# A transformer block with routed experts on one core: the router's logits taken from rows before their norm, with a shift row fetched by way of DRAM

## The reference, cut to what matters

```python
    mod = (jax.nn.silu(c) @ w_ada + b_ada)[:, None, :]
    sh1, sc1, gt1, sh2, sc2, gt2 = jnp.split(mod, 6, axis=-1)
    ...
    merged = jax.nn.sigmoid(ga) * (ya @ w_branch_a) + jax.nn.sigmoid(gbm) * (yb @ w_branch_b)
    x = x + gt1 * (merged @ w_out)
    h2 = _rmsnorm(x, norm2_g) * (1.0 + sc2) + sh2
    x = x + gt2 * _moe(h2, router_w, router_b, w_gate_up, b_gate_up, w_down, b_down)
```

```python
    logits = (xt @ router_w + router_b).astype(jnp.float32)
    top_v, top_e = lax.top_k(logits, TOP_K)          # 4 of 32 experts
    wts = jax.nn.softmax(top_v, axis=-1)
    ...
        hgu = xb @ w_gate_up[e] + b_gate_up[e]
        gate, up = jnp.split(hgu, 2, axis=-1)
        ...
        return act @ w_down[e] + b_down[e]
    out = jax.ops.segment_sum(ys * pw[:, None].astype(ys.dtype), ptok, num_segments=N + 1)[:N]
```

## Time and profile before

| | us |
|---|---|
| median of 3 runs | 1346.19 |
| lowest and highest | 1345.65, 1347.37 |
| the profiled execution's own time | 1347.94 |
| its span | 1346.2 |
| TensorE busy | 1320.4 (98%) |
| GpSimd busy | 703.6 (52%) |
| VectorE busy | 478.4 (36%) |
| ScalarE busy | 300.9 (22%) |
| HBM read | 482.40 MB, 359 GB/s over the span |

### The profile page before, as it was taken

How to read it: one execution, slowest core, us unless ns; L and a number is a source line. 1 busy time by engine, 2 the same in 40 slices (tenths; PEclk the granted TensorE clock), 3 DMA queues, 4 the chain that set the end, 5 groups by cost and what they waited for, 6 DMA issues and landing times.

```text
span 1346.2 us, 18076 instructions
## 1 busy us (share of the span) xinstructions
PE 1320.4 (98%) x6683; PEld 620.1 (46%) x6684; DVE 478.4 (36%) x862; ACT 300.9 (22%) x577; POOL 703.6 (52%) x430
## 2 busy tenths in 40 slices
PE   7999999999999999999999999999999999999996
PEld 3888545788844333333333333333333333333332
DVE  1160006355578324223233242333332333233332
ACT  2320004310023222222122122222222222222222
POOL 1000000010015777767777687777777777777771
PEclk9999999999999999999999999999999999999998
DMA  9735333499959999999999999999999999999995
GB/s 339 279 127 186 125 125 125 161 322 367 329 219 382 429 428 429 428 403 429 428 428 428 428 409 429 428 428 428 407 431 428 428 428 407 430 428 428 428 427 231
DMA packets 70818, 483.79 MB, mean 359 GB/s; under 512 B 7270, under 2 KB 7466, under 8 KB 44970
## 3 DMA queue, kind: packets, MB, share of 16 engines
q1 hardware_dynamic: 69250, 478.20, 86.8%
q0 software_dynamic: 1056, 3.93, 1.0%
q10 hardware_dynamic: 488, 1.33, 0.3%
HBM read 482.40 MB, written 1.05 MB: 359 GB/s over the span
## 4 chain that ended last, share of the span: by engine, by line
DMA 56%; PE 34%; POOL 4%; issue 3%; DVE 1%; SPq 1%; ACT 1%; POOLq 0%; DVEq 0%; ACTq 0%
DMA landing<-in_w_gate_up 41%; PE bank L1332 15%; DMA landing<-in_w_down 14%; PE bank L1341 6%; POOL gu_slot L566 3%; PE bank L1688 3%; PE bank L1738 3%; PE bank L1574 2%; DMA piece<-in_w_ada 2%; SPq L397 1%; PE bank L1660 1%; PE bank L1553 0%; PE bank L1478 0%; PE bank L1705 0%; SPq L391 0%
## 5 line engine op out<-in xcount | busy, mean ns | idle before, releaser
L566 POOL COPY gu_slot<-landing 128x2048 f32<-128x2048 f32 x246 | 458.8, 1895 | 145.0 <-issue 107.9
L1688 PE MATMUL bank<-gu_slot,xg 128*64 128x512 f32 x2304 | 509.4, 593 | 3.2 <-POOL gu_slot L566 2.8
L1688 PEld LDWEIGHTS bank<-gu_slot,xg 128*64 128x64 f32 x2304 | 164.3, 137 | 320.5 <-issue 298.4
L566 POOL COPY dn_slot<-landing 128x2048 f32<-128x2048 f32 x120 | 223.5, 1894 | 71.2 <-issue 53.6
L1738 PE MATMUL bank<-dn_slot,actT 128*64 128x512 f32 x1152 | 255.1, 595 | 0.0
L1332 PE MATMUL bank<-hT,piece 128*128 128x256 f32 x704 | 153.4, 379 | 0.0
L1738 PEld LDWEIGHTS bank<-dn_slot,actT 128*64 128x64 f32 x1152 | 79.5, 137 | 159.2 <-issue 158.7
L1332 PEld LDWEIGHTS bank<-hT,piece 128*128 128x128 f32 x704 | 133.4, 190 | 19.1 <-issue 1.1
L812 ACT ACTIVATE ypart<-bank 128x512 bf16<-128x512 f32 x105 | 62.7, 597 | 313.8 <-DVE bank L1241 260.2
L1230 DVE TENSOR_SCALAR bank<-bank 128x512 f32<-128x512 f32 x36 | 25.2, 700 | 283.6 <-PE bank L1688 283.6
L1241 DVE SCALAR_TENSOR_TENSOR bank<-bank,slot_w,gt2q 128x512 f32<-128x512 f32 x35 | 26.6, 759 | 238.8 <-PE bank L1738 238.8
(11 more groups left out here) (342 smaller groups left out, 986.8 us busy)
## 6 DMA issues: line engine op xcount, KB each, us to landing
landing<-in_w_gate_up SPq DMA_DIRECT2D x123, 2048.0 KB, 10.7
landing<-in_w_down SPq DMA_DIRECT2D x60, 2048.0 KB, 10.7
piece<-in_w_in SPq DMA_DIRECT2D x17, 2048.0 KB, 7.7
piece<-in_w_ada SPq DMA_DIRECT2D x12, 2048.0 KB, 13.2
gu_slot<-in_w_gate_up SPq DMA_DIRECT2D x10, 1024.0 KB, 7.1
dn_slot<-in_w_down SPq DMA_DIRECT2D x8, 1024.0 KB, 13.8
piece<-in_w_branch_a SPq DMA_DIRECT2D x2, 2048.0 KB, 9.3
piece<-in_w_branch_b SPq DMA_DIRECT2D x2, 2048.0 KB, 8.1
```

Of the source, the lines that this page charges most:

```text
L566: nc.gpsimd.tensor_copy(place, landing[j // 2 % 3][:, j % 2, :]).then_inc(there, 16)
L1688: ins = M(gu_bank[u][64 * q:64 * q + 64, :], xg[:, k % 4, 64 * (k // 4):64 * (k // 4) + 64], gu_slot[k][:, cols_], start=(k == 0), stop=(k ...
```

## The change

Three things are changed together.

1. The logits. TensorE transposes `u`, the row times `sc2g` before the norm (for the first tile a buffer of its own, `u0`), and multiplies it with the router's weights. VectorE multiplies the outcome with 1/rms and adds `cb`, a row of 32 numbers that is the same for all tokens: the shift row sh2 times the router's weights, plus the router's bias. For `cb` GpSimd writes sh2 (one row) to DRAM and reads it back with one element per partition and column (`shc`); TensorE forms the row `hc` from it in the place of `ab6`, and repeats it on all partitions beside the gate sum.
2. The gate row gt2 is formed in one tile (`ab7`) with its two 512-wide halves on the two halves of the partitions, straight into `gt2q`; `gt2`, `ab6` and GpSimd's two copies go. `bd`, the down biases, is kept in that form too and is half as wide.
3. The order. VectorE clears most of its buffers and splits the first tile ahead of the last w_out tile (two of the clearings go to GpSimd); the first block's ranks come in two tiles of their own (`rank0_full`, `rank1_full`), its selection for each token tile apart; the second tile's `h2` is formed behind the logits; `chosen2` of the first block ahead of the router weights, both of which stand behind `br`; the second tile's first subtraction behind the places, its second behind `table`. The products nobody reads are spread over other waits. SyncE's unit 0 waits for the second logits, unit 1 for `h2`; the first two landing buffers change places.

The diff, cut to its core:

```diff
-    + [("wb2", "V"), ("wb3", "V"), ("ab6", "V"), ("wo0", "V"), ("wo2", "V"), ("ab7", "V"), ("wo1", "V"), ("wo3", "V")]
-    + [("hh0", "A"), ("hh1", "A"), ("rp0", "A"), ("rl0", "V"), ("hh2", "A"), ("hh3", "A"), ("rp1", "A"), ("rl1", "V"), ...
+    + [("wb2", "V"), ("wb3", "V"), ("hc", "V"), ("wo0", "V"), ("wo2", "V"), ("ab7", "V"), ("wo1", "V"), ("wo3", "V")]
+    + [("hh2", "A"), ("hh0", "A"), ("hh1", "A"), ("hh3", "A"), ("rp0", "A"), ("rl0", "V"), ("rp1", "A"), ("rl1", "V"), ...
...
 SyncE
+            wait_tile(sp, "rl1")
+            land(E - 1, 0)
             sp.wait_ge(h2_ready, 4)
-            sp.wait_ge(gate_ready, 3)
-            land(E - 1, 0)
-            wait_tile(sp, "rl1")
+            sp.wait_ge(gate_ready, 1)
             land(E - 1, 1)
...
 GpSimd
+            wait_out(pool, "ab3")
+            pool.dma_start(shift_store[:], sh2[0:1, :]).then_inc(shift_out, 16)
+            pool.wait_ge(shift_out, 16)
+            pool.dma_start(shc[:], shift_store[0].rearrange("(k p) -> p k", p=P), allow_slow_non_contiguous=True).then_inc(shc_in, 16)
...
-            for q in range(2):
-                step.settle()
-                step(nc.gpsimd.tensor_copy(gt2q[64 * q:64 * q + 64, :], gt2[64 * q:64 * q + 64, 512 * q:512 * q + 512]), gate_ready)
-            step(nc.gpsimd.tensor_tensor(bd[:], bd[:], gt2[:], ALU.mult), gate_ready)
+            step(nc.gpsimd.tensor_tensor(bd[:], bd[:], gt2q[:], ALU.mult), gate_ready)
+            wait_tile(pool, "wo3")
+            for i in range(2):
+                step(nc.gpsimd.memset(ypart[i][:], 0.0), ypart_ready[i])
...
 VectorE
             weigh(7)
-            take_sum(6)
             take_wo(0)
             take_wo(2)
-            take_sum(7)
-            second_norm(0)
+            take_gate()
+            dve.wait_ge(row_full, 1)
+            step(V.tensor_copy(cb[:], tile("hc")[:, 64:64 + E]), row_out)
+            step.settle()
+            norm_scale(0)
+            norm_rows(0)
...
-                chain(V.tensor_copy(lg[:, t, 0:E], tile(f"rl{t}")[:, 0:E]), out_dve)
+                chain(V.scalar_tensor_tensor(lg[:, t, 0:E], tile(f"rl{t}")[:, 0:E], rs[:, t:t + 1], cb[:], ALU.mult, ALU.add), out_dve)
...
-            router_weights(0)
+            dve.wait_ge(rank0_full, 1)
+            first_slots(0, bank[6][:, 0:1])
+            norm_rows(1)
+            dve.wait_ge(rank1_full, 1)
+            first_slots(1, bank[5][:, 0:1])
             wait_tile(dve, "rt")
...
-            router_weights(1)
+            chosen_of_slots(first_slot[:, 0:1], first_slot[:, 1:2])
             wait_tile(dve, "br")
...
-            subtract_part(0, 1)
+            router_weights(0)
+            router_weights(1)
...
-            subtract_part(1, 1)
+            subtract_part(0, 1)
...
             chain(V.tensor_copy(table[:], tile("te")[0:1, 0:ends[5]]), tables_ready)
+            subtract_part(1, 1)
...
 TensorE
+            pe.wait_ge(late_in, 48)
+            pe.wait_ge(shc_in, 16)
+            ps = begin("hc")
+            for k in range(KT):
+                M(ps[0:1, 0:E], shc[:, k:k + 1], wr[:, k, :], start=(k == 0), stop=False)
+            full(M(ps[0:1, 0:E], ones[0:1, 0:1], rb[:], start=False, stop=True))
             pe.wait_ge(merged_ready, 4)
...
                 if t == 0:
-                    add_parts(7)
+                    add_gate_parts()
+                    wait_out(pe, "hc")
+                    M(tile("hc")[:, 64:64 + E], ones[0:1, :], rb2[:], start=True, stop=True).then_inc(row_full, 1)
...
+            pe.wait_ge(u_ready, 3)
+            transposes("hh2", h2, 1, 0)
+            pe.wait_ge(row_out, 1)
+            transposes("hh0", u0, None, 0)
+            transposes("hh1", u0, None, 1)
+            wait_out(pe, "wo2")
+            keep_busy(bank[7], 4)
+            pe.wait_ge(u_ready, 4)
+            transposes("hh3", h2, 1, 1)
...
-            gate_up(16, 1, (block_tables, weight_transposes))
+            gate_up(16, 1, (weight_transposes, block_tables))
```

More of the change, by code:

```diff
@@ L500, in _ @@
             pool.dma_start(sc2g[:], norm2_g[0:1, :].to_broadcast([P, D])).then_inc(g2_in, 16)
-            for part, dst in ((2, gt1), (3, sh2), (5, gt2), (4, fgb)):
+            for q in range(2):
+                a = 5 * D + 512 * q
+                pool.dma_start(gt2b[64 * q:64 * q + 64, :], b_ada[0:1, a:a + 512].to_broadcast([64, 512])).then_inc(brow_in, 16)
+            for part, dst in ((2, gt1), (3, sh2), (4, fgb)):
                 pool.dma_start(dst[:], b_ada[0:1, part * D:(part + 1) * D].to_broadcast([P, D])).then_inc(brow_in, 16)
@@ L1129, in _ @@
             step(V.memset(selT[:], 0.0), selw_out)
-            for i in range(3):
-                step(V.memset(ypart[i][:], 0.0), ypart_ready[i])
+            step(V.memset(ypart[2][:], 0.0), ypart_ready[2])
             step(V.memset(zrow[:], 0.0), zrow_ready)
+            subtract_part(1, 0)
             dve.wait_ge(numbers_ready, 1)
             step(V.tensor_scalar(esel[:], ones[0:3 * E, 0:SLOTS], expert_no[:], None, ALU.is_gt), esel_ready)
+            take_wo(3)
+            norm_scale(1)
             step(V.memset(lg[:, :, E:E + TOP_K], PAD))
@@ L1547, in _, with add_gate_parts @@
             attend(3)
+            def add_gate_parts():
+                ps = begin("ab7")
+                pe.wait_ge(modq_ready, 8)
+                for q in range(2):
+                    ins = M(ps[64 * q:64 * q + 64, :], ones[:, 0:64], modq[q][:], start=True, stop=True)
+                full(ins)
             def add_parts(r):
```

132 lines of the change are left out of this document (70 added, 62 removed), and 2 rows, old and new, of the table PLAN.

## The result

| | kernel before | changed kernel |
|---|---|---|
| median (15 runs each), us | 1346.92 | 1348.94 |
| lowest and highest | 1345.56, 1349.54 | 1346.94, 1350.56 |
| the profiled execution's own time | 1347.94 | 1347.66 |
| its span | 1346.2 | 1346.0 |

The ratio is 1.0015, interval 1.0008 to 1.0022, which is 2.0 us (1.1 to 3.0). A second measurement, further down, gives 1.0009 (1.0000 to 1.0018), medians 1.4 us apart. The forecast was 1.3 us more than before.

A forecast was written before the change was run, and what follows sets the result against it. The weight stream sets the pace, with TensorE beside it up to 580 us. The later of stream (+1.3 us) and TensorE (+0.5) gave +1.3 us on a median of 1346.19: 1347.5 us, range 1343.9 to 1349.9.

The forecast's parts named there:

- Part 1: Up to the last w_out product: `hc` for `ab6` costs nothing; the row's broadcast product adds 0.15 us to TensorE.
- Part 2 and 3: Router chain and VectorE's row: second logits at 406.0 us, router weights 415.3 against 414.71, `left` 417.65 against 416.12.
- Part 4: GpSimd's copies: the second tile's second subtraction holds the second copy; unit 3 and `pick` come 1.3 us later.
- the sum: Whole kernel: the later of the stream (unit 2 +0.2, unit 3 +1.3 us) and TensorE (+0.5): +1.3 us; chance 0.68.
- the rule of 2.7 us ahead: Weight stream: a request keeps it full if made 2.7 us before the one ahead has landed.
- TensorE +1.3 less 0.76 of slack: +0.5: TensorE's path into the loop: +1.3 us for `pick`, less 0.76 us of slack at 580 us, gives +0.5 us.
- The subtraction for nothing: Rival at GpSimd's first copies: the second subtraction costs nothing, unit 2's +0.2 us remains, 1346.4 us; chance 0.10.
- The holes: Rival, faster: units 2 and 3 requested earlier fill the stream's two holes, about 1.3 us each, 1342.9 us; chance 0.08.
- The shift row: Rival, slower: GpSimd's trip of `sh2` through DRAM, 19 us by the rows, is late before w_out; 1366 us; chance 0.04.
- the crowd of waits: Rival, slower: several VectorE and GpSimd waits around the copies and `pick` at once, +3.0 us, 1349.2 us; chance 0.10.

The follow-up runs named there:

- the first experiment: The changed kernel with the second tile's second subtraction replaced by clearing its result; ratio 1.0004 (0.9994 to 1.0013) against the kernel before.

## Why the prediction was right, point by point

**The time.** Forecast +1.3 us, traces +1.23 and +1.09, medians +2.0 and +1.4. 1347.5 was said, the first measurement gave 1348.94, 0.7 us of which is that the kernel before too was 0.7 us above the three runs from which I started.

**Part 1** was mis-sized: +0.15 said, +0.68 found. The row's product costs 0.33 us, not 0.15: the next product starts that much behind it; and I took the two halves of the gate sum for one sum, where four products take 1.01 us for two in 0.86; 0.2 us more lie in the w_out products themselves. `hc` before w_out was rightly put at nothing: w_out begins 16.22 us behind the anchor in both.

**Part 2 and 3.** Counted behind the anchor of before, the second logits were forecast at 51.2 us, the end of the weights at 60.5, of `left` at 62.85, unit 2 at 62.95; measured 51.5, 60.7, 62.76, 62.83. The logits fit by luck in part: w_out ended 0.5 us later than said, and the chain behind it was that much shorter. The first gate_up was forecast at 59.1 us and came at 59.92, without consequence, since the first copy waited for GpSimd's rounding. VectorE's row did become the bound, laid end to end from rows of the kernel before. Unit 2's slack was measured by itself, 1.34 us.

**Part 4.** `left` holds a rounding step (1.40 us): that was one end of the range; of 63.6 to 64.5 us for the first copy I took 63.9, and it was the late end, 64.45. The second copy is held 1.0 us, by the subtraction, as said, and not the 1.25 us of the sum. Unit 3: 68.95 forecast, 69.20 measured. `pick`: 76.8 and 76.72.

The split of unit 3's delay was less right than its size. Of the 1.3 us, 0.2 were to come from a later first copy and 1.1 from the subtraction between the copies; of the 1.55 us measured, 0.75 lie before the first copy, which is the 0.77 us by which the router weights are done later, and 0.80 between there and the request. Without the subtraction 0.1 us of the cost is left at the end, and 0.56 of 1.33 us in "stream"; with the subtraction put back in its old place about 1.0 of 1.33 us stays, since there it holds the first copy for 0.6 us, and the first copy is no earlier. So it takes both, the weights that are ready later and a subtraction that falls among the copies. That the later weights cost their 0.75 us is read from the trace; the runs that moved the weights forward changed TensorE's order too and do not isolate it.

That unit 3 alone decides was wrong: a later copy held costs as much, and the rule of 2.7 us ahead, from which unit 4 was taken to be early enough, did not hold. The size came out right since the change holds the copy for unit 3.

**The sum.** "TensorE +1.3 less 0.76 of slack: +0.5" was wrong in both terms, with no effect on the sum. TensorE entered the loop 0.67 us later, because in the kernel before it used `pick` only 0.62 us after it was there; and its slack was 26.40 - 25.32 = 1.08 us.

**The rivals.** The subtraction for nothing is refuted by the first experiment and by the copy of 2.90 us. The holes were not filled; none of the kernels tried did it. The shift row took 10 us, not the 19 of the rows, and was 26 us early; one trip of 4 KB took about 5 us in this stretch, where the queues moved 383 GB/s (333 to 338 us). The Trainium skill's rule ("DMA: Bandwidth & Descriptors", Anatomy of one DMA, SWDGE path), from which an estimate of 4 us for both trips followed, was too cheap. Of the crowd of waits one came, `left` on the rounding, within the range given for it.

## What to carry to other kernels

Where GpSimd copies set the pace of a stream, look for the full-width VectorE operations that fall among them. Here one of 1.2 us held a copy for 1.0 us, at either of two places behind the first copy, and for 0.5 to 0.7 us where part of it fell into a pause that GpSimd had anyway. A chain shortened by 1.6 us on one engine was worth nothing, since what the copies wait for came 0.75 us later. Taking an operation out shows what the operation costs, and only putting it back shows what its place costs: here 1.12 and about 0.4 us. Read the slack of a path from the distance between equal steps of two blocks, not from the longest wait in a row. And count from an anchor behind the noisy part of the program: here the spans of two profiles had the opposite sign of the medians. Repeat one trace, too, before reading tenths from two.

## What the runs showed of the hardware that was not expected

**Where the spread of the runs comes from.** The same code up to 53 us took 1.43 us longer in the profile of before. Its stretches, then those of the changed kernel:

```profile
20.00:30.00 10.00, 8.82 (x60) 4.66 (x62) 2.89 (x11) 0.60 (x1) 0.00 (x0) 0.90 1.01 323
30.00:40.00 10.00, 9.85 (x45) 5.68 (x38) 1.84 (x7) 2.48 (x6) 0.00 (x0) 0.76 1.03 380
```

```profile
20.00:30.00 10.00, 9.17 (x62) 5.01 (x64) 2.67 (x11) 0.60 (x1) 0.00 (x0) 0.92 1.01 325
30.00:40.00 10.00, 9.85 (x52) 6.31 (x42) 2.06 (x8) 3.83 (x10) 0.00 (x0) 0.91 1.04 385
```

The clock missing is 1.0 + 2.4 = 3.4 us in the first and 0.8 + 0.9 = 1.7 us in the second; at half clock (the 1.2 GHz level) that is 6.8 and 3.4 us. All fourteen profiles show one of these two amounts: over 20 to 40 us the mean granted clock is 0.91 in ten and 0.83 in four. From 40 to 1320 us it is full in all of them but for the three places above. With 3.4 us missing the anchor lies at 354.1 to 354.8 us (four profiles), with 1.7 at 352.75 to 353.7 (nine); one with 1.7 lies at 354.6, and its products between 18 and 26 us already ran 2.1 us later than in the profile of before. From 40 us to the anchor nothing more is added: each profile keeps there the distance that it has to the profile of before. So up to the anchor the profiles differ by as much as 2.05 us, more than this change is worth, and all of it is there within the first 40 us; the larger amount goes with an anchor that is about 1 us later on average. The page's clock line shows a 9 there all the same, in slices of 34 us, and so the prediction's first reading, full clock in all slices but the last, passed over it. The executions of one kernel, run beside each other, spread over 1.4 to 5.3 us; that they differ for the same reason is likely, but not shown.

**The clock behind a wait.** Three traces show TensorE at half clock near the router, behind waits of 0.91, 0.74 and 2.07 us; two traces of the changed kernel have a wait of 1.17 and 1.19 us for `pick` and keep full clock, and so do the kernel with the subtraction behind the slot numbers (1.28 us) and that with the fillers ahead of the ranks (1.58 us). The length of the wait alone does not tell them apart. What it costs was measured: 1.6 us for eight products, 2.2 us at the end, and products nobody reads in the wait gave it back.
